# An encoder layer in float32 pairs: a row norm's spreading one step later, two idle PSUM banks for one branch product, and a tail with one turn per tile

## The reference

```python
h = rms_norm(x, pre_g);  u = h @ w_in          # columns split among branches A, B, C and 3 merge gates
ya = rms_norm(diff_attention(aq, ak, av), subln_g) * 0.8 * silu(ag)     # 4 heads, two softmax maps each
yb = gqa_attention(rope(norm(bq)), rope(norm(bk)), bv) * silu(bg)       # 8 query heads, 2 kv heads
yc = neighbourhood_attention(cq, ck, cv, rpb) * silu(cg)                # 8 heads
m = g0 * (ya @ wa) + g1 * (yb @ wb) + g2 * (yc @ wc)                    # g = sigmoid(merge gates)
x = x + rms_norm(m @ w_out, post_g)
x = x + sigmoid(x @ w_pg) * (p @ w_pe)                                  # "embedding", p is 256 wide
```

## Time and profile before

| | us |
|---|---|
| median of 3 runs (1511.76 to 1512.51) | 1512.39 |
| the profiled execution's own time | 1514.99 |
| its span, first to last instruction | 1513.2 |
| PE busy | 1400.8 (93%) |
| DVE busy | 607.8 (40%) |
| ACT busy | 542.7 (36%) |
| POOL busy | 290.9 (19%) |

### The profile page before, as it was taken

The page is one execution under the profiler, slowest core; times in us unless marked ns, Lnnn a source line. Parts: engine busy times, 40 slices in busy tenths (PEclk is TensorE's granted clock), DMA queues, the critical chain, the costliest instruction groups (busy, mean ns, idle before and its releaser), DMA issues.

```text
span 1513.2 us, 18374 instructions
## 1 busy us (share of the span) xinstructions
PE 1400.8 (93%) x6780; PEld 1132.8 (75%) x6780; DVE 607.8 (40%) x1089; ACT 542.7 (36%) x1000; POOL 290.9 (19%) x180
## 2 busy tenths in 40 slices
PE   4999999889999798987999898989898999899998
PEld 3787777678887575765788786878787888788887
DVE  4355555556100636456212115162525212544332
ACT  4354454443111536445211115252524212324432
POOL 1221112212222113020022131211211112213100
PEclk9999999999999999999999999999999999999999
DMA  4211101101111000000011110111100113322200
GB/s 172 71 36 37 45 28 50 45 29 45 42 43 55 28 14 28 14 14 8 22 42 57 61 56 16 54 34 35 34 28 29 42 42 139 112 83 71 69 35 35
DMA packets 25753, 71.87 MB, mean 47 GB/s; under 512 B 2872, under 2 KB 4792, under 8 KB 25568
## 3 DMA queue, kind: packets, MB, share of 16 engines
q1 hardware_dynamic: 25696, 71.09, 14.5%
HBM read 66.86 MB, written 4.23 MB: 47 GB/s over the span
## 4 chain that ended last, share of the span: by engine, by line
PE 71%; DVE 5%; ACT 2%; issue 2%; POOL 0%; DVEq 0%; ACTq 0%
PE ps L639 34%; PE ps L906 9%; PE ps L701 6%; PE ps L1098 6%; PE ps L1080 6%; PE ps L686 3%; PE ps L679 2%; PE ps L658 2%; PE ps L666 2%; PE ps L1104 1%; ACT s L1166 1%; DVE pt_lo L1580 1%; ACT pt_hi L1178 0%; DVE s L1635 0%; DVE s L1610 0%
## 5 line engine op out<-in xcount | busy, mean ns | idle before, releaser
L492 POOL TENSOR_TENSOR w_lo<-stage,w_hi 128x1024 fp32r<-128x1024 f32 (+1 forms) x92 | 193.2, 2100 | 864.2 <-ACT w_hi L1151 863.9
L639 PE MATMUL ps<-h_hi,w_hi 128*128 128x512 f32 x768 | 243.4, 398 | 2.0 <-ACT s L1166 1.8
L639 PE MATMUL ps<-h_lo,w_hi 128*128 128x512 f32 x768 | 237.8, 391 | 0.0
L639 PE MATMUL ps<-h_hi,w_lo 128*128 128x512 f32 x768 | 237.3, 390 | 0.0
L1151 ACT CAST w_hi<-stage 128x1024 fp32r<-128x1024 f32 (+1 forms) x92 | 86.0, 935 | 310.9 <-PE ps L639 222.1
L639 PEld LDWEIGHTS ps<-h_lo,w_hi 128*128 128x128 f32 x768 | 144.7, 188 | 31.0
L639 PEld LDWEIGHTS ps<-h_hi,w_hi 128*128 128x128 f32 x768 | 140.1, 188 | 36.8 <-issue 8.8
L639 PEld LDWEIGHTS ps<-h_hi,w_lo 128*128 128x128 f32 x768 | 144.4, 188 | 30.8
L1580 DVE TENSOR_TENSOR pt_lo<-ps,pt_hi 128x512 fp32r<-128x512 f32 (+2 forms) x160 | 91.3, 603 | 105.2 <-ACT pt_hi L1178 99.1
L658 PE MATMUL ps<-h_hi,w_hi 128*128 128x512 f32 x272 | 113.1, 416 | 0.0
L658 PE MATMUL ps<-h_lo,w_hi 128*128 128x512 f32 x272 | 108.5, 399 | 0.0
(11 more groups left out here) (214 smaller groups left out, 2394.7 us busy)
## 6 DMA issues: line engine op xcount, KB each, us to landing
stage<-in_w_gates SPq DMA_DIRECT2D x24, 512.0 KB, 3.3
stage<-in_w_qkvg_a SPq DMA_DIRECT2D x19, 512.0 KB, 6.0
stage<-in_w_qkvg_c SPq DMA_DIRECT2D x16, 512.0 KB, 3.3
stage<-in_w_branch SPq DMA_DIRECT2D x24, 256.0 KB, 2.6
m<-in_x_tok SPq DMA_DIRECT2D x4, 1024.0 KB, 11.1
y<-in_x_tok SPq DMA_DIRECT2D x8, 512.0 KB, 3.5
stage<-in_w_pg SPq DMA_DIRECT2D x16, 256.0 KB, 2.7
out<-y SPq DMA_DIRECT2D x16, 256.0 KB, 2.0
```

What stands on the lines that cost most here:

```text
L492: nc.gpsimd.tensor_tensor(dst, stage[:, slot, 0:width], f32(hi), ALU.subtract).then_inc(w_ready, 1)
L639: done = mm(ps[:, bank + g, :], w[:, slot, k * P:(k + 1) * P], h[:, k, g * SEQ:(g + 1) * SEQ], start=first and part == 0, stop=last and pa ...
```

## The change

Three edits.

1. Branch A: `spread_rstd` moves from steps t = 6 and 2 to t = 7 and 3, `norm_y` too; `make_diagonal` stays in t = 6 and 2, behind `half_lo` and `max_a`.
2. Merges: the product of f = 6 goes into banks 0 and 1 and waits only for the merge's first sum; f = 7 waits for the sum of f = 5. The turn of the rope buffer into bank 0 behind merge 0 waits for the sum of f = 6.
3. Tail: the sixteen embeddings are written out in the order `EMBEDS`. Six tiles (`KEPT`) keep their turned parts in six slots (the two old ones and chunks 4 to 7 of `h_hi` and `h_lo`), tiles 6 and 7 reuse the first two. Each tile is turned once, straight from the residual; the copies are gone. Right half weights are due at the seventh embedding instead of the ninth, and are brought two chunks for each of the first four embeddings.

```diff
+KEPT = 6
+EMBEDS = [(t, 0) for t in range(KEPT)] + [(0, 1), (1, 1), (6, 0), (6, 1), (7, 0), (7, 1)] \
+    + [(t, 1) for t in range(2, KEPT)]
+FIRST_USE = [EMBEDS.index((t, 0)) for t in range(TILES)]
+        x2t = [(hi[:, :], lo[:, :]) for hi, lo in lhs] + [(h_hi[:, k, :], h_lo[:, k, :]) for k in range(4, KC)]
+        def branch_bank(f):
+            return 0 if isinstance(f, int) and f == KC - 2 else 2
...
# SP, tail
+            for e in range(len(EMBEDS)):
+                if 1 <= e < KC // 2:
+                    for c in range(2):
+                        load_w(N_PG[1] + 2 * e + c, c, w_pg[KC + 2 * e + c])
+                store(e)
...
# PE, between_a
-                if t == 6 or t == 2 and i:
-                    spread_rstd(2 * i if t == 6 else 2 * i - 1)
+                if t == 7 or t == 3 and i:
+                    spread_rstd(2 * i if t == 7 else 2 * i - 1)
...
# PE, merge_branch
-                pe.wait_ge(merged, LEAD + b * KC + f)
+                if isinstance(f, int) and f == KC - 1:
+                    pe.wait_ge(merged, LEAD + b * KC + KC - 2)
+                elif branch_bank(f):
+                    pe.wait_ge(merged, LEAD + b * KC + f)
+                else:
+                    pe.wait_ge(merged, LEAD + b * KC + 1)
-                            done = mm(ps[:, 2 + g, :], w[:, slot, c * P:(c + 1) * P],
+                            done = mm(ps[:, branch_bank(f) + g, :], w[:, slot, c * P:(c + 1) * P],
...
             pe.wait_ge(roped, LEAD + 2)
+            pe.wait_ge(merged, LEAD + KC - 1)
             turn(rope_buf, 0, rope_turned)
...
# PE, tail
-            def turn_x2(t, c):
-                pe.wait_ge(x2_copied, LEAD + t + 1)
+            def turn_x2(t):
+                pe.wait_ge(x2_ready, LEAD + t + 1)
                 pe.wait_ge(x2_split, LEAD + t - 1)
-                turn(copy_of_x[c], 4 + 2 * c, x2_turned)
+                turn(x_row(t), 4 + 2 * (t % 2), x2_turned)
...
+            for e in range(len(EMBEDS)):
+                if e == 0 or e == KEPT:
+                    half = e // KEPT
+                    pe.wait_ge(w_ready, LEAD + N_PG[half] + KC)
+                    pe.wait_ge(w_ready, LEAD + N_PE + 2)
+                if e + 1 in FIRST_USE:
+                    turn_x2(FIRST_USE.index(e + 1))
+                embed(e)
...
# ACT, tail
+                if t >= KEPT:
+                    act.wait_ge(pe_done, LEAD + EMBEDS.index((slot, 1)) + 1)
+                to_hi(x2t[slot][0], 4 + 2 * (t % 2), 1.0, x2_hi_done)
...
-            def copy_x2(half, i, c):
-                act.wait_ge(x2_ready, LEAD + (TILES if not isinstance(i, int) or i or half else c + 1))
-                act.wait_ge(x2_turned, LEAD + half * TILES + 2 * i + c - 1)
-                nc.scalar.copy(copy_of_x[c], m_tile(2 * i + c)).then_inc(x2_copied, 1)
...
# DVE, step_a
-                if t % 4 == 2 and c >= 0:
-                    make_diagonal(c)
                 half_lo(T - 1)
                 if T + 2 < TILES_A:
                     max_a(T + 2)
+                if t % 4 == 2 and c >= 0:
+                    make_diagonal(c)
...
-                if t % 4 == 2 and c >= 0:
+                if t % 4 == 3 and c >= 0:
                     norm_y(c)
```

More of the change, by code:

```diff
@@ L122, in build_program @@
         lambda_in = tables[:, 256:256 + 4 * HD]
-        copy_of_x = [tables[:, c * TOK:(c + 1) * TOK] for c in range(2)]
         neg_half = small[:, 0:1]
@@ L449, in _, with store @@
                 load_w(N_PE + c, c, w_pe[c])
[L451 to L454, removed]
+            def store(e):
+                t, half = EMBEDS[e]
+                sp.wait_ge(o_ready, LEAD + e + 1)
+                sp.dma_start(out[t][:, half * 512:(half + 1) * 512], o_tile(e % 2)).then_inc(o_stored[e % 2], 16)
             for c in range(2):
                 load_w(N_PG[1] + c, c, w_pg[KC + c])
[L458 to L466, removed]
+            for e in range(len(EMBEDS)):
[3 more added lines that the diff above has]
+                store(e)
             for c in range(2):
@@ L617, in _ @@
                 out_tile(TILES // 2 - 1, c, c == 1)
[L618 to L622, removed]
+            for k in range(KC):
+                cols = slice(k * 512, (k + 1) * 512)
+                split_w(N_PG[1] + k, k % 2, dst=pg_parts[1][1][:, cols], width=512, hi=pg_parts[1][0][:, cols])
         @block.tensor
@@ L1103, in embed @@
                     for part, (a, w) in enumerate([(p_hi, w_hi), (p_hi, w_lo), (p_lo, w_hi)]):
-                        done = mm(ps[:, 2 + c, :], a[:, (2 * c + k) * P:(2 * c + k + 1) * P],
+                        done = mm(ps[:, 2 + c, :], a[:, (2 * slot + k) * P:(2 * slot + k + 1) * P],
                                   w[:, k, half * 512:(half + 1) * 512],
@@ L1114, in _ @@
             out_tile(TILES // 2 - 1, 0)
-            turn_x2(0, 0)
+            turn_x2(0)
             out_tile(TILES // 2 - 1, 1)
             pe.wait_ge(x2_ready, LEAD + TILES - 1)
[L1118 to L1130, removed]
+            for e in range(len(EMBEDS)):
[6 more added lines that the diff above has]
+                embed(e)
         @block.scalar
@@ L1531, in out_tile, with turned_hi @@
                     .then_inc(r_sq, 1)
-            def turned_hi(half, i, c):
-                t = half * TILES + 2 * i + c
+            def turned_hi(t):
+                slot = t % KEPT
                 act.wait_ge(x2_turned, LEAD + t + 1)
-                act.wait_ge(r_done, LEAD + TILES - 1 + (0 if isinstance(t, int) and t == 0 else 1))
-                act.wait_ge(pe_done, LEAD + t - 1)
-                to_hi(lhs[c][0][:, :], 4 + 2 * c, 1.0, x2_hi_done)
+                act.wait_ge(r_done, LEAD + TILES - (1 if t == 0 else 0))
+                if t >= KEPT:
+                    act.wait_ge(pe_done, LEAD + EMBEDS.index((slot, 1)) + 1)
+                to_hi(x2t[slot][0], 4 + 2 * (t % 2), 1.0, x2_hi_done)
@@ L1539, in turned_hi, with embed @@
                 act.wait_ge(p_in, 16)
-                nc.scalar.copy(p_hi[:, c * 256:(c + 1) * 256], p_raw[:, bass.ds((2 * i + c) * 256, 256)]) \
+                nc.scalar.copy(p_hi[:, slot * 256:(slot + 1) * 256], p_raw[:, t * 256:(t + 1) * 256]) \
                     .then_inc(p_hi_done, 1)
[L1543 to L1553, removed]
+            def embed(e):
+                c = e % 2
+                if e + 1 in FIRST_USE:
+                    turned_hi(FIRST_USE.index(e + 1))
+                if e < KC // 2:
+                    for k in range(2):
+                        split_w(N_PG[1] + 2 * e + k, k, N_PG[1] // 2 + e + 1,
+                                dst=pg_parts[1][0][:, (2 * e + k) * 512:(2 * e + k + 1) * 512], width=512)
+                act.wait_ge(pe_done, LEAD + e + 1)
+                act.wait_ge(o_ready, LEAD + max(e - 1, 0))
@@ L1838, in merge_add @@
                 by_tile = lambda ap: ap.rearrange("p (t q) -> p t q", t=TILES)
+                product = banks(branch_bank(f))
                 if b == 0:
-                    stt(out=m_f, in0=by_tile(s_row(c)), scalar=1.0, in1=by_tile(banks(2)), op0=ALU.add,
+                    stt(out=m_f, in0=by_tile(s_row(c)), scalar=1.0, in1=by_tile(product), op0=ALU.add,
                         op1=ALU.mult).then_inc(merged, 1)
                 else:
-                    steps.done(dve, stt(out=s_row(c), in0=s_row(c), scalar=1.0, in1=banks(2), op0=ALU.add,
+                    steps.done(dve, stt(out=s_row(c), in0=s_row(c), scalar=1.0, in1=product, op0=ALU.add,
                                         op1=ALU.mult))
@@ L2083, in out_tile, with turned_lo, embed @@
                 nc.vector.tensor_tensor(m_tile(2 * i + c), s_row(c), y[:, c, :], ALU.add).then_inc(x2_ready, 1)
-            def turned_lo(half, i, c):
-                t = half * TILES + 2 * i + c
+            def turned_lo(t):
+                slot = t % KEPT
                 dve.wait_ge(x2_hi_done, LEAD + t + 1)
-                sub(lhs[c][1][:, :], banks(4 + 2 * c), lhs[c][0][:, :]).then_inc(x2_split, 1)
+                sub(x2t[slot][1], banks(4 + 2 * (t % 2)), x2t[slot][0]).then_inc(x2_split, 1)
                 dve.wait_ge(p_hi_done, LEAD + t + 1)
[L2090 to L2097, removed]
+                cols = slice(slot * 256, (slot + 1) * 256)
+                sub(p_lo[:, cols], p_raw[:, t * 256:(t + 1) * 256], p_hi[:, cols]).then_inc(p_split, 1)
+            def embed(e):
+                t, half = EMBEDS[e]
+                c = e % 2
+                if e + 1 in FIRST_USE:
+                    turned_lo(FIRST_USE.index(e + 1))
+                dve.wait_ge(e_tanh, LEAD + e + 1)
                 steps.done(dve, stt(out=e_tile(c), in0=e_tile(c), scalar=1.0, in1=ps[:, 2 + c, :], op0=ALU.add,
                                     op1=ALU.mult))
-                dve.wait_ge(o_stored[c], LEAD + 16 * (half * (TILES // 2) + i))
-                stt(out=o_tile(c), in0=e_tile(c), scalar=0.5, in1=m_tile(2 * i + c)[:, half * 512:(half + 1) * 512],
+                dve.wait_ge(o_stored[c], LEAD + 16 * (e // 2))
```

(1 more changed line is left out.)

18 lines of the change are left out of this document (8 added, 10 removed).

## The result

The changed kernel takes 1467.68 us (median of 4 runs, 1464.75 to 1469.95) against 1512.45 (4 runs, 1511.76 to 1512.82): a ratio of 0.9703, 95% interval 0.9685 to 0.9722, so 44.8 us less. The forecast was 1466.0, with a range of 1459 to 1479. The profiled execution took 1469.95 us of its own, forecast 1468.9; its span is 1468.0, against 1513.2 before.

A forecast was written before the change was run, and what follows sets the result against it. PE, busy 93% of the span, was taken as the bound. Gains 30.3 + 1.7 + 7.15 + 0 + 7.0 = 46.1 us took the span from 1513.2 to 1467.1 and the median to 1466, range 1459 to 1479.

The forecast's parts named there:

- Part 1: Branch A: seven waits before the spreading and the lower clock behind them go, 30.3 us.
- the doubtful third: Branch A: the clock's part of the 30.3 us; the waits alone, without it, were 19.7 us.
- The two things that could be late next: Branch A: diagonal before the spreading, 2 us to spare; norm before the next mix, 1.5 us to spare.
- Part 2: Merges: products of f = 6 and f = 7 follow without a wait; 1.7, 7.15 and 0 us for merges 0, 1, 2.
- Merge 0 and merge 1: Wait before the last branch product and its slow products go: 1.7 us and 7.15 us.
- Merge 2: The wait only moves ahead of the output tiles, some 4.2 us, ended by `first_lo`; 0, ends -1.6 and +0.9.
- Part 3: Tail: sixteen turns become eight, each costing 0.87 us on PE, 7.0 us gained.
- The norm on the mix: Rival, branch A: six of seven mixes wait 0.4 us and lose 1.77 in clock, 13 us, 1479; chance 0.12.
- The tail with its old spacing: Rival, tail: embeddings still 7.69 us apart because another engine is as slow, 7.0 us more, 1473; chance 0.04.
- slow instruction supply: Rival, tail: straight code comes late; at 3.5 us lost per embedding, 10 us slower than before, 1522; chance 0.03.
- The clock elsewhere: Rival, branches B and C: slow stretches fewer (1459, chance 0.10) or more (1473, chance 0.06).

The follow-up runs named there:

- e7_merge2_as_before: Changed kernel with only merge 2 put back (f = 6 in banks 2 and 3, f = 7 waiting for its sum): 1465.52 us, ratio 0.9691.
- e2: Kernel before with the second edit (merges) alone: 1503.16 us, ratio 0.9938 to the kernel before.
- e5: Kernel before, with PE running products nobody reads while it waits for the diagonal: 1504.78 us against 1512.78, ratio 0.9941.
- e6_diagonal_first: Changed kernel with the diagonal back at the head of DVE's step, spreading still a step later: 1473.95 us, ratio 0.9739 to the kernel before.

## Why the prediction was right

The size was off by 1.7 us in 1467.7, and by 0.9 in the profiled span. The terms came out one by one, but that 0.9 is partly luck: the first stage gave 1.1 more than forecast, and branch B, where nothing was forecast, took 1.8 back.

**Part 1** (forecast 30.3). Alone it gave 30.2. All of the waits' time went, and with it the part in the clock, which was the doubtful third: filling the waits recovered 8.0 to 8.9 us of it. The two things that could be late next have nearly the room that I gave them: the diagonal 3.1 us instead of 2 (its four operations took 0.88, not 1.0, and DVE came to them earlier), the norm 1.6 instead of 1.5. What I did not see is that two things were moved, with two gains: some 24 us from the later spreading and, once that is done, 6 from the diagonal's new place behind the maxima (the new place without the later spreading was not run). I had written that the maxima come earlier than before and counted nothing for it. The sum was right because it was taken from the spacing of PE's turns, which holds both.

**Part 2.** Merge 0 and merge 1 came out at 1.7 and 7.16. Merge 2 was taken as 0 within -1.6 and +0.9; the two stages around it sum to +0.5, of which 0.2 lies behind the merge's first branch product, as `e7_merge2_as_before` shows. The new wait is where it was forecast, 4.3 us instead of 4.2, with `first_lo` ending 0.1 before the tile begins. The profile names its releaser "issue", not DVE: only DVE's timeline shows whom PE waited for.

**Part 3** (7.0). 7.1 in the chain, 7.3 alone, and 7.1 back again when eight turns were added.

**The rivals.** The norm on the mix: no wait of PE there in any profile. The tail with its old spacing, and slow instruction supply: embeddings 6.80 apart, sixteen written out one by one. The clock elsewhere came true in small. Branch C has four slow stretches, each with a clock of 0.77 over 15 us, before (from 925, 997, 1068 and 1140 us) and after (from 885, 957, 1028 and 1100), and its share is within 0.3 us. Branch B took 243.89 us in the profile after and 242.08 before. It has five slow stretches in both. Over 20 us each, from 494.4, 520, 580, 645 and 685 us, the clock was 0.91, 0.83, 0.83, 0.91 and 0.83 before; from 458, 490, 550, 613 and 656 us it was 0.83, 0.83, 0.83, 0.91 and 0.83 after. One of the five is deeper after: an estimate of 20 x 0.08 = 1.6 us from these clocks, nearly the whole 1.8. It doesn't follow the edits: B's work is the same in all ten kernels and took 239.7 (e2) to 243.9 us (the change, and e5, which has none of the three edits). The runs show the same. The change's four spread over 5.2 us, the fastest (1464.75) at a mean granted clock of 0.980, the slowest (1469.95) at 0.977, and 0.003 of 1467 is 4.4. The kernel before spreads over 1.1 in these four runs, but over 3.9 and 3.5 in the two later sets of nine. Why the clock falls differently from run to run is open.

## What to carry to other kernels

Price a short wait of TensorE by the starts of the same work before and after it, not by its idle time: here some 9 of the 30 us that seven waits cost were the slow clock behind them, and products that nobody reads won 8 to 9 back. When an instruction is moved, follow who is queued behind it on each engine: the diagonal's place was worth 6 us through two other engines, at a wait that the kernel before did not show. A wait that moves instead of going (merge 2) says what to change next: ask which half of the operand is late, and do the other half first.

## What the runs showed of the hardware

The same four diagonal operations on DVE took 0.88 us alone and 3.01 us when they met POOL's weight split: in `e6_diagonal_first` POOL's operation ran from 119.53 to 121.93, and the first of the four, begun at 119.60, ended at 122.0. The Trainium skill ("SBUF — State Buffer", section "SBUF: two separate sides") says of the pair of ports that VectorE and GpSimd share: whichever starts first, a GpSimd operation or a VectorE operation in a two-port mode, gets the pair for the whole instruction, and the other fully blocks. 3.01 against 0.88 agrees; in which mode the four ran, no run here shows.

Useless products in a wait made the kernel faster by 8.0 us at a wait that was no shorter, with the granted clock up from 0.97 to 1.00 in that branch. A wait of 4.3 us ahead of the output tiles cost 6.0 there, at a clock of 0.86 over the 12 us around it.
